# One conditional pass of a mixture-of-experts kernel moves from the middle of the expert units to behind them

## What is computed

```python
def moe(h, router_w, router_b, w1, b1, w2, b2):
    logits = (h @ router_w + router_b).astype(jnp.float32)
    top_v, top_i = lax.top_k(logits, TOP_K)          # 4 of 32 experts
    gates = jax.nn.softmax(top_v, axis=-1)
    ...
    def expert_block(args):
        xb, e = args
        hid = xb @ w1[e] + b1[e]                      # 1024 -> 2048
        return clamped_swiglu(hid[:, :D_FF], hid[:, D_FF:]) @ w2[e] + b2[e]   # 1024 -> 1024
    ...
    contrib = ys[dest] * gate_sorted[:, None]
    return jax.ops.segment_sum(contrib, tok_sorted, num_segments=T)

x = x + gf * moe(hf, ...)
return rmsnorm(x, final_norm_w)      # then the second block starts with its own rmsnorm
```

## Time and profile before

| | us |
|---|---|
| median of 3 runs | 1993.76 (1990.1 to 1995.72) |
| the profiled execution | 1995.57 |
| its span in the profile | 1993.7 |
| TensorE busy | 1752.5 (88%) |
| VectorE, ScalarE, GpSimd busy | 440.4, 280.8, 114.5 |
| HBM read and written | 538 MB and 7.6 MB, 274 GB/s over the span |

### The profile page before, as it was taken

How to read it: one execution, slowest core, us unless ns; L and a number is a source line. 1 busy time by engine, 2 the same in 40 slices (tenths; PEclk the granted TensorE clock), 3 DMA queues, 4 the chain that set the end, 5 groups by cost and what they waited for, 6 DMA issues and landing times.

```text
span 1993.7 us, 20775 instructions
## 1 busy us (share of the span) xinstructions
PE 1752.5 (88%) x8422; PEld 1053.4 (53%) x8422; DVE 440.4 (22%) x1011; ACT 280.8 (14%) x569; POOL 114.5 (6%) x258
## 2 busy tenths in 40 slices
PE   6999999597998787868799959699998999899997
PEld 3535675142343233424244414277776788688885
DVE  2135221011111111112011201232456622211101
ACT  4023321011011010001001101012222210100000
POOL 1000000000000000000046600000020000000000
PEclk9999999797999898989899969799998999999999
DMA  9225356999998999889999999963434325344340
GB/s 378 104 87 220 132 203 237 420 419 414 417 417 371 419 415 412 329 337 418 410 419 416 417 420 419 410 249 117 152 132 143 119 71 190 125 151 169 113 161 21
DMA packets 135845, 547.01 MB, mean 274 GB/s; under 512 B 10109, under 2 KB 23549, under 8 KB 99774
## 3 DMA queue, kind: packets, MB, share of 16 engines
q1 hardware_dynamic: 129200, 529.83, 67.0%
q0 software_dynamic: 3200, 11.01, 1.5%
q10 hardware_dynamic: 3342, 4.77, 0.7%
HBM read 537.97 MB, written 7.60 MB: 274 GB/s over the span
## 4 chain that ended last, share of the span: by engine, by line
PE 73%; DMA 15%; SPq 5%; DVE 3%; ACT 2%; issue 1%; ACTq 0%; DVEq 0%
PE PS L1138 15%; DMA ring<-in_w 7%; PE PS L1154 7%; DMA arena<-in_w 6%; SPq L1623 5%; PE PS L2151 4%; PE PS L2161 4%; PE PS L2153 4%; PE PS L1995 3%; PE PS L2016 3%; PE PS L2008 3%; PE PS L1134 3%; PE PS L1166 3%; PE PS L1108 3%; PE PS L497 2%
## 5 line engine op out<-in xcount | busy, mean ns | idle before, releaser
L1138 PE MATMUL PS<-ring,arena 128*32 128x512 f32 (+2 forms) x1272 | 320.8, 674 | 67.2 <-DMA ring<-in_w 33.7
L1138 PE MATMUL PS<-arena 128*32 128x512 f32 (+2 forms) x776 | 222.0, 666 | 25.4 <-DMA ring<-in_w 20.8
L1138 PEld LDWEIGHTS PS<-ring,arena 128*32 128x32 f32 (+2 forms) x1272 | 100.0, 141 | 242.6 <-issue 242.6
L1154 PE MATMUL PS<-ring,arena 128*32 128x512 f32 (+2 forms) x600 | 155.2, 733 | 34.5 <-DMA ring<-in_w 21.8
L1154 PE MATMUL PS<-arena 128*32 128x512 f32 (+2 forms) x424 | 132.9, 732 | 34.9 <-DMA ring<-in_w 20.0
L1425 DVE TENSOR_SCALAR arena<-PS 128x512 f32<-128x512 f32 x28 | 19.2, 687 | 537.0 <-PE PS L1138 537.0
L1138 PEld LDWEIGHTS PS<-arena 128*32 128x32 f32 (+2 forms) x776 | 68.7, 143 | 126.3 <-issue 126.2
L1154 PEld LDWEIGHTS PS<-ring,arena 128*32 128x32 f32 (+2 forms) x600 | 46.4, 148 | 113.1 <-issue 112.1
L1154 PEld LDWEIGHTS PS<-arena 128*32 128x32 f32 (+2 forms) x424 | 41.0, 156 | 108.5 <-issue 107.5
L2151 PE MATMUL PS<-arena,ring 128*128 128x256 f32 x352 | 82.7, 390 | 6.6 <-DVE arena L2290 6.6
L1995 PE MATMUL PS<-arena,ring 128*128 128x256 f32 x384 | 84.6, 380 | 0.0
(11 more groups left out here) (430 smaller groups left out, 2043.2 us busy)
## 6 DMA issues: line engine op xcount, KB each, us to landing
ring<-in_w SPq DMA_DIRECT2D x234, 1024.0 KB, 18.6
arena<-in_w SPq DMA_DIRECT2D x150, 1024.0 KB, 18.9
ring<-in_w_ada SPq DMA_DIRECT2D x24, 1024.0 KB, 7.6
ring<-in_w_in SPq DMA_DIRECT2D x22, 1024.0 KB, 13.6
ring<-in_w_up SPq DMA_DIRECT2D x20, 1024.0 KB, 9.6
ring<-in_w_gate SPq DMA_DIRECT2D x16, 1024.0 KB, 6.7
ring<-in_w_down SPq DMA_DIRECT2D x11, 1024.0 KB, 7.0
ring<-in_w_out SPq DMA_DIRECT2D x8, 1024.0 KB, 4.9
```

The source lines that it names most:

```text
L1138: m = pe.matmul(bank(("up", i, b))[rows[n], :], xs[:, k, rows[n]], tiles[n][:, b * 512:(b + 1) * 512], start=False, stop=k == 7, skip_grou ...
L1154: m = pe.matmul(bank(("down", i, c))[rows[n], :], actT[:, k, rows[n]], tiles[n][:, a:a + 512], start=k == 0, stop=k == 7, skip_group_check ...
```

## The change

The two lists become one, `MAIN_STEPS`, over all 14 units, so the pipeline runs through from unit 6 to unit 7, and the side steps stand in unit 7 too. The `If` of every engine stands behind the last unit, ahead of the second block; GpSimd gets one as well. What the body waits for, and its additions to `xv`, are inside the body, which is not entered. In the last `down` VectorE evicts both halves, one after the other, and ScalarE none. In every `scatter` the wait for the two halves is taken apart: the first two groups of matmuls wait for the first half, the other two for the second.

```diff
@@ expert_steps
-            if hi == len(MAIN_UNITS):
+            if sort[8]:
                 yield from [s for one in side for s in one]
                 yield ("early",)
@@ plan
-        HEAD_STEPS = list(expert_steps(0, CUT, SIDE, SORT))
-        plan_experts(EXPERTS, plan, HEAD_STEPS)
-        HEAD_N, HEAD_USES, HEAD_LOADS = plan.n, list(plan.uses), len(plan.loads)
-        TAIL_STEPS = list(expert_steps(CUT, len(MAIN_UNITS), SIDE, PLAIN))
-        plan_experts(EXPERTS, plan, TAIL_STEPS)
-        MAIN_N, MAIN_USES = plan.n, list(plan.uses)
+        MAIN_STEPS = list(expert_steps(0, len(MAIN_UNITS), SIDE, SORT))
+        plan_experts(EXPERTS, plan, MAIN_STEPS)
+        MAIN_N, MAIN_USES, MAIN_LOADS = plan.n, list(plan.uses), len(plan.loads)
@@ tensor_experts, scatter
-                    for c in range(2):
-                        w.wait_ge(x.moved[g_of["down", i, c].bank], g_of["down", i, c].use)
                     w.wait_ge(x.spread, i + 1)
                     for c in range(4):
+                        w.wait_ge(x.moved[g_of["down", i, c // 2].bank], g_of["down", i, c // 2].use)
                         room(g_of["y", i, c])
@@ scalar_experts, down
-                    w.wait_ge(x.pe_done, g.n)
-                    act.activation(ysr[:, 512:1024], bank(("down", i, 1)), ACT.Copy).then_inc(x.moved[g.bank], 1)
+                    if not x.first or i < LAST:
+                        w.wait_ge(x.pe_done, g.n)
+                        act.activation(ysr[:, 512:1024], bank(("down", i, 1)), ACT.Copy).then_inc(x.moved[g.bank], 1)
@@ vector_experts, down
                     dve.tensor_copy(ysr[:, 0:512], bank(("down", i, 0))).then_inc(x.moved[g.bank], 1)
+                    if x.first and i == LAST:
+                        g = g_of["down", i, 1]
+                        dve.tensor_copy(ysr[:, 512:1024], bank(("down", i, 1))).then_inc(x.moved[g.bank], 1)
@@ tensor (the same on vector, scalar and sync)
-            tensor_experts(pe, w, EXPERTS, HEAD_STEPS)
+            tensor_experts(pe, w, EXPERTS, MAIN_STEPS)
             w.wait_ge(most_ready, 1)
             with pe.If(pe.value_load(most[0:1, 0:1], min_val=0, max_val=512) > S):
                 ...
-            tensor_experts(pe, w, EXPERTS, TAIL_STEPS)
             tensor_post(pe, w)
@@ vector, inside the body
+                mine.count(dve.memset(yacc, 0.0))
...
+                for j in range(8):
+                    dve.scalar_tensor_tensor(out=xv[:, j, :], in0=yacc[:, j, :], scalar=mods[:, 40 + j, 0:1], in1=xv[:, j, :], op0=ALU.mult, op1=ALU.add).then_inc(more_added, 1)
@@ gpsimd
             pool_experts(pool, w, own, EXPERTS)
+            w.wait_ge(most_ready, 1)
+            with pool.If(pool.value_load(most[0:1, 0:1], min_val=0, max_val=512) > S):
+                inside = Waits(pool)
+                all_done(inside, MORE)
+                inside.wait_ge(more_added, 8)
             pool_post(pool, w, own)
```

More of the change, by code:

```diff
@@ L973, in build @@
         SORT[0], SORT[1], SORT[8] = [("softmax",)], [("permute",)], [("b2",)]
-        CUT, LAST = 7, len(MAIN_UNITS) - 1
+        LAST = len(MAIN_UNITS) - 1
         def plan_experts(x, p, steps):
@@ L1629, in first_done @@
         def first_done(w):
-            w.wait_ge(pe_done, HEAD_N)
+            w.wait_ge(pe_done, MAIN_N)
             for b in range(8):
-                w.wait_ge(moved[b], HEAD_USES[b])
+                w.wait_ge(moved[b], MAIN_USES[b])
         def experts_done(w):
@@ L1675, in build @@
         fin_ready, fin_square, fin_root = sem("fin_ready"), sem("fin_square"), sem("fin_root")
+        more_added = sem("more_added")
         norm_done = sem("norm_done")
@@ L2589, in vector @@
             vector_route(dve, w, own)
-            vector_experts(dve, w, own, EXPERTS, HEAD_STEPS)
+            vector_experts(dve, w, own, EXPERTS, MAIN_STEPS)
             w.wait_ge(most_ready, 1)
@@ L2594, in vector @@
                 first_done(inside)
-                vector_experts(dve, inside, Order(inside, dve_own_more), MORE, MORE_STEPS)
+                mine = Order(inside, dve_own_more)
+                mine.count(dve.memset(yacc, 0.0))
+                mine.wait()
+                vector_experts(dve, inside, mine, MORE, MORE_STEPS)
                 all_done(inside, MORE)
@@ L2598, in vector @@
                     inside.wait_ge(MORE.moved[b], more.uses[b])
-            vector_experts(dve, w, own, EXPERTS, TAIL_STEPS)
+                for j in range(8):
+                    dve.scalar_tensor_tensor(out=xv[:, j, :], in0=yacc[:, j, :], scalar=mods[:, 40 + j, 0:1], in1=xv[:, j, :], op0=ALU.mult, op1=ALU.add).then_inc(more_added, 1)
+                inside.wait_ge(more_added, 8)
             vector_post(dve, w, own)
@@ L2607, in scalar @@
             scalar_route(act, w)
-            scalar_experts(act, w, own, EXPERTS, HEAD_STEPS)
+            scalar_experts(act, w, own, EXPERTS, MAIN_STEPS)
             w.wait_ge(most_ready, 1)
@@ L2614, in scalar @@
                 all_done(inside, MORE)
-            scalar_experts(act, w, own, EXPERTS, TAIL_STEPS)
+                inside.wait_ge(more_added, 8)
             scalar_post(act, w, own)
@@ L2630, in sync @@
             sp.dma_start(ctxT, I["ctxT"].rearrange("(k p) t -> p k t", p=128)).then_inc(ctx_in, 16)
-            load_all(sp, w, plan.loads[:HEAD_LOADS], pe_done, slot_in)
+            load_all(sp, w, plan.loads[:MAIN_LOADS], pe_done, slot_in)
             w.wait_ge(most_ready, 1)
@@ L2637, in sync @@
                 all_done(inside, MORE)
-            load_all(sp, w, plan.loads[HEAD_LOADS:], pe_done, slot_in)
+            load_all(sp, w, plan.loads[MAIN_LOADS:], pe_done, slot_in)
             w.wait_ge(norm_done, 9)
```

## The result

| | before | after |
|---|---|---|
| median, us | 1995.62 (15 runs, 1990.1 to 1998.79) | 1988.8 (15 runs, 1985.38 to 1993.47) |
| the profiled execution | 1995.57 | 1988.99 |
| its span | 1993.7 | 1987.2 |

The ratio is 0.9968 with a 95% interval of 0.9959 to 0.9977: 6.4 us less than before (4.6 to 8.2). The prediction was 5.8 us less, inside a range of 11.3 less to 0.3 more.

What follows compares the result with a forecast made beforehand. DMA was taken to bound the expert units and TensorE the second block. The terms -14.5 + 3.8 + 4.9 = -5.8 us gave a median of 1988.0 us, range 1982.5 to 1994.0.

Steps and rivals of the forecast that it cites:

- What bounds the units: In the expert units, time is bytes over DMA rate plus the DMA engines' standstill when all 13 slots are full.
- Term 1: Unit 7 without the branch: unit 8's first up comes sooner, 66.3 us instead of 80.9 after unit 5's down; -14.5 us.
- Term 2: GpSimd's tables start one unit sooner, so unit 11 gets its DMA standstill back; +3.8 us, bounds 0 and 5.5.
- Term 3: Branch between last scatter and second block: TensorE's uncovered jump +3.2 us and low clock +1.7 us, together +4.9 us.
- The covers: Jumps of ScalarE, VectorE, SP and GpSimd and two new table loads hide behind other work; they cost nothing.
- The sum: All three terms together, for the whole kernel: -5.8 us, giving a median of 1988.0 us.
- The hidden jump: Rival: the jump behind the last unit is hidden, so only terms 1 and 2 count; -10.7, 1983.1 us, chance 0.12.
- Unit 7 and unit 11 lose nothing: Rival: the whole 20.6 us of standstill come back, nothing given back in unit 11; -15.7, 1978.1 us, chance 0.08.
- The gain goes where the DMA engines stop next: Rival: unit 7 keeps some 10 us of standstill, unit 11 gets 5.5; -0.2, 1993.6 us, chance 0.15.
- Slower: Rival: unit 7's standstill stays, leaving only the jump and the clock; +4.9, 1998.7 us, chance 0.05.

Runs made afterwards that it cites:

- the second profile: The changed kernel run again unchanged for another profile: 1988.7 us.
- the fastest kernel: The changed kernel with TensorE's and ScalarE's conditions turned round and no side steps in unit 7: 1981.62 us, ratio 0.9931 to the kernel before.
- joint wait: The changed kernel, but every scatter waits for both halves of the down at once again: 1988.01 us, ratio 0.9963 to the kernel before.
- ScalarE evicting: The changed kernel, but ScalarE evicts the second half of the last down again: 1986.8 us, ratio 0.9957 to the kernel before.

## Why the prediction was right

It was right in its sign and nearly in its size, with two terms off by 1.8 to 2.6 us in opposite directions.

- **What bounds the units** held. The standstill fell by 13.3 us and the units by 13.4.
- **Term 1**, -14.5 us: the distance was to fall from 80.9 to 66.3 us and was measured at 66.3, the standstill left at 6.3 against 6.1. The equal piece of program around unit 11 was the right measure. The run with two lists and no branch showed what the prediction had not parted: 8.1 us of it are the branch with the low clock behind it, 6.4 the drain of the pipeline.
- **Term 2**, +3.8 us, was mis-sized: 1.2 in the stretch, and 1.1 by the experiment. The step that failed is that, because the four rounds "end about when unit 11 begins", their writes all fall into units that are full of DMA. The rounds did end there: the fourth pair of writes is issued at 1050.84, and the `down` that answers to the one at 1062.65 in the earlier trace rows starts at 1052.11. But issued is not landed: that pair landed 8 to 12 us into unit 11. Its 1.05 MB take 2.5 us of DMA time, and 3.8 - 2.5 = 1.3, near the 1.2 measured. That the size comes from this is an estimate; no run moved that pair alone.
- **Term 3**, +4.9 us, was 6.7 against the run without a branch. The later start was +3.4 us where +3.2 stood, and the load did wait for VectorE's second copy, as assumed. The low clock right behind the standstill was +1.7 us, as stated (8.83 against 7.14). So the two parts that the prediction named measured 5.1 us together. What was left out is a stretch at 1.2 GHz some 10 us later, in L1976 and the third set: +1.0 and +0.6 us. It came again in the second profile, but it is not shown to be the branch's. The kernel before has part of it (its third set takes 5.39 us, 3.70 at the full clock), the fastest kernel has more of it without any standstill (21.9 us to L1982), and with the same jump it is shorter or gone where other work stands ahead (no side steps in unit 7: 25.1 us to L1982; joint wait: 23.7). In these traces the clock falls in or right behind L1976, 32 matmuls of only two columns each; what sets it is open. The branch behind the last unit thus cost between 3.5 us (23.7 - 20.2, joint wait) and 6.9 us (27.1 - 20.2, ScalarE evicting) in the traces, counted from the last scatter.
- **The covers** held. ScalarE's jump was over long before its work, VectorE's first instruction (1316.67) is behind the jump and waits for TensorE, SyncE's branch at 1272.4 is followed by the next load at 1277.66, and the two table loads cost nothing as long as TensorE is held: removing TensorE's branch alone brought 1.3 us of them to light. The second one stayed hidden too: L1982 starts when the third set ends. With the third set at the full clock (joint wait) VectorE's last instruction ahead of it ends 0.3 us before L1983 starts, so the cover just held.
- **The sum**: -14.5 + 3.8 + 4.9 = -5.8 was, in what was measured, -14.5 (unit 7) + 1.2 + 6.7 = -6.6 (span -6.5, by the ratio of the runs -6.4). The misses of 2.6 and 1.8 us went in opposite directions, so that the total is within 0.8 us is in part luck.
- **The rivals.** The hidden jump would have given -10.7; TensorE's row of 6273 ns and its start 7.9 us behind the scatter exclude it, and it lies outside the 4.6 to 8.2 us of the timed runs. The Trainium skill's 108 ns for a compare-and-branch (page "Advanced Engine Details and Errata", section "Control Flow Timing") is near what TensorE shows when the branch isn't taken, 89 ns; for the jump over the pass's code it is off by 6.2 us. The Trainium skill's page "Runtime: NRT & Kernel Launch", section "Instruction fetch mechanics", names the reason for such a difference, the fetch of a target that is not at hand. The run with the condition turned round agrees with it, 89 ns against 6273, and so do ScalarE's two instruction packets, which are gone when its branch isn't taken; for TensorE the fetch itself is in no row. "Unit 7 and unit 11 lose nothing" is excluded by the 6.3 and 1.2 us that they still lose, "The gain goes where the DMA engines stop next" by the same two numbers, where it had 10 and 5.5, and "Slower" by 6.3 us instead of 20.6 in unit 7.

## What to carry to other kernels

A branch that was jumped in the middle of an engine's work cost that engine 5 to 7 us here, and TensorE 1.7 to 2.2 us more by its low clock behind it (the last figure from its gather in unit 7, 6.08 us instead of 3.84). Where nothing covers that, turn the condition until the case that happens is the code that follows, even at the price of writing the program behind it twice. Here that gave back all 6.7 us of the profile, on the engine where it mattered and with the table loads on ScalarE, and the timed interval lies below the changed kernel's (0.9921 to 0.9951 against 0.9959 to 0.9977). And where DMA is the limit, price a gap on another engine by the standstill of the DMA engines in its stretch (GB/s against the full rate), and look for writes of side work that fill such gaps: they are worth leaving where they are (1.1 us here).

## What the runs showed of the hardware

- TensorE's compare is recorded with 89 ns when it isn't taken and with 6.3 us when it jumps over some thousand rows. On ScalarE the row is short either way (50 ns when it jumps; 49 ns where it isn't taken, with the condition turned round, and 38 ns for the jump at that arm's end), on VectorE it is 72 ns when it jumps, and there the jump shows only as time without issue behind it: 5.5 us on VectorE and 5.5 us on ScalarE (6.0 with the load and the compare). A short row of a compare says nothing of what the branch cost.
- The length of TensorE's jump is not one number: 3.4 to 3.8 us at the end of its work (the three runs with the condition turned round), 5.1 us with matmuls queued ahead, 6.2 before, 6.3 in the changed kernel (twice), 6.8 and 6.9 us where the load went out 0.1 us behind the scatter's start. In the last two the instruction queue q8 has two packets during the jump, in the ones of 6.2 and 6.3 us one. What makes the difference is open.
- Where the two arms of a branch meet, the program's list has two more table loads on ScalarE (1.28 us each), and none where the following code stands inside the arm.
- After a standstill of 4.2 us the granted clock of TensorE's next 3.7 us was 0.61, after one of 2.1 us the first set ran at the full clock, and a second low stretch came some 10 us later in an engine that had been busy throughout. The second one does not need the first: in the fastest kernel it follows a standstill of 0.8 us and a set at the full clock.
